# Token columns of the second block multiplied by Strassen-like pairs on the unnormalised input

## The reference, cut to what matters

```python
for l in range(2):
    x = x + 0.5 * swiglu(rms_norm(x, ffn1_norm[l]), ffn1_w_gate[l], ffn1_w_up[l], ffn1_w_down[l])
    u = rms_norm(x, mix_norm[l])
    (a_q, a_k, a_v, b_x, b_b, b_c, c_q, c_kc, c_vc, c_ks, c_vs, c_kw, c_vw, c_g,
     d_q, d_k, d_v, d_g, gate_logits) = jnp.split(u @ w_in[l], SPLIT_POINTS, axis=-1)
    # sliding-window attention (a), short convolution (b), block-sparse attention (c), retention (d)
    ...
    x = x + merged @ w_out[l]
    x = x + 0.5 * swiglu(rms_norm(x, ffn2_norm[l]), ...)
```

## Time and profile before

| | before |
|---|---|
| median of 3 runs | 2752.19 us |
| the profiled execution | 2756.73 us |
| its span on the core | 2754.9 us |
| TensorE busy | 2544.6 us, 92% |
| VectorE busy | 990.4 us, 36% |
| ScalarE busy | 431.9 us, 16% |
| TOK of layer 0 | 1365.90 to 1444.36 us |
| TOK of layer 1 | 2161.39 to 2239.85 us |

### The profile page before, as it was taken

The page is one execution under the profiler, slowest core; times in us unless marked ns, Lnnn a source line. Parts: engine busy times, 40 slices in busy tenths (PEclk is TensorE's granted clock), DMA queues, the critical chain, the costliest instruction groups (busy, mean ns, idle before and its releaser), DMA issues.

```text
span 2754.9 us, 33930 instructions
## 1 busy us (share of the span) xinstructions
PE 2544.6 (92%) x14163; PEld 1950.3 (71%) x14163; DVE 990.4 (36%) x2007; ACT 431.9 (16%) x964; POOL 57.3 (2%) x65
## 2 busy tenths in 40 slices
PE   7998888888878888899999999999999999999999
PEld 5784444444435444588898788888888897788888
DVE  1421100010000001366523522767666325515665
ACT  2321101010111001111012420110110113401110
POOL 0000000000000000100010000000000010000000
PEclk9986877787887788799999999999999999999999
DMA  9657999999999999954565344545544555255440
GB/s 357 241 195 326 420 428 429 428 429 428 428 428 429 428 429 428 380 175 161 154 170 169 106 123 139 182 168 168 172 165 168 154 155 168 80 156 176 154 168 16
DMA packets 250735, 694.43 MB, mean 252 GB/s; under 512 B 11024, under 2 KB 193664, under 8 KB 225536
## 3 DMA queue, kind: packets, MB, share of 16 engines
q1 hardware_dynamic: 248160, 688.54, 67.0%
q10 hardware_dynamic: 2464, 4.32, 0.4%
HBM read 691.78 MB, written 1.05 MB: 251 GB/s over the span
## 4 chain that ended last, share of the span: by engine, by line
PE 84%; DMA 12%; DVE 2%; ACT 1%; issue 1%; SPq 1%; POOL 0%; DVEq 0%
PE banks L1278 11%; DMA ring<-in_w 11%; PE banks L1659 8%; PE banks L1182 7%; PE banks L1198 6%; PE banks L926 4%; PE banks L1742 4%; PE banks L1169 4%; PE banks L1468 3%; PE banks L1335 3%; PE banks L1331 3%; PE banks L1333 3%; PE banks L1337 3%; PE banks L1338 3%; PE banks L1327 3%; PE banks L1329 3%
## 5 line engine op out<-in xcount | busy, mean ns | idle before, releaser
L1169 PE MATMUL banks<-ring,BK 128*32 128x512 f32 x2048 | 274.8, 678 | 127.8 <-DMA ring<-in_w 115.5
L1169 PEld LDWEIGHTS banks<-ring,BK 128*32 128x32 f32 x2048 | 64.8, 117 | 321.9 <-issue 153.9
L1659 PE MATMUL banks<-ZT,ring 128*128 128x256 f32 x1024 | 232.3, 380 | 0.1
L1659 PEld LDWEIGHTS banks<-ZT,ring 128*128 128x128 f32 x1024 | 192.8, 190 | 28.6 <-issue 3.6
L1198 PE MATMUL banks<-ring,GB 128*32 128x512 f32 x976 | 148.9, 754 | 0.0
L1182 PEld LDWEIGHTS banks<-cst,PB 128*128 128x128 f32 x512 | 92.3, 278 | 44.8 <-ACT QT L1931 44.8
L1742 PE MATMUL banks<-YT,ring 128*128 128x256 f32 x512 | 117.3, 380 | 0.0
L1182 PE MATMUL banks<-cst,PB 128*128 128x32 f32 x512 | 94.9, 353 | 24.1 <-DVE QT L2445 24.1
L2445 DVE COPY QT<-banks 128x512 f32<-128x512 f32 x32 | 20.6, 686 | 263.2 <-PE banks L1169 263.2
L926 PE MATMUL banks<-ring,ZT 128*128 128x256 f32 (+2 forms) x576 | 112.4, 358 | 0.0
L1182 PE MATMUL banks<-cst,QT 128*128 128x32 f32 x512 | 111.6, 393 | 0.0
(11 more groups left out here) (460 smaller groups left out, 4004.1 us busy)
## 6 DMA issues: line engine op xcount, KB each, us to landing
ring<-in_w SPq DMA_DIRECT2D x189, 2048.0 KB, 20.3
ring<-in_w_in SPq DMA_DIRECT2D x71, 1024.0 KB, 5.2
ring<-in_ffn_w_gate SPq DMA_DIRECT2D x44, 1024.0 KB, 5.5
ring<-in_ffn_w_up SPq DMA_DIRECT2D x44, 1024.0 KB, 7.8
ring<-in_ffn_w_down SPq DMA_DIRECT2D x44, 1024.0 KB, 5.5
ring<-in_w_mod SPq DMA_DIRECT2D x24, 1024.0 KB, 11.6
ring<-in_w_out SPq DMA_DIRECT2D x12, 1024.0 KB, 5.0
ring<-in_w_branch SPq DMA_DIRECT2D x8, 1024.0 KB, 5.7
```

The source lines that it names most:

```text
L1169: last = mm(ps[32 * j:32 * j + 32, 4 + b, :], XE[:, k, :], slot(n)[:, 512 * b:512 * b + 512], start=(k < 4), stop=(k >= 4))
L1659: last = mm(out, slot(n)[:, 256 * k + P * (c % 2):256 * k + P * (c % 2) + P], ZT[:, k, :], start=(k == 0), stop=(k == KC - 1))
```

## The change

The 12 TOK tiles become six pairs with seven products, like those of an FFN, on the unnormalised input ZG. The pairs are two tiles of one width: 256, 256, 256, 218, 218 and 216. So

- TensorE makes 28 matmuls a pair; the first pair goes through `by_chunks`, the others through the new `tokens(j)`. Both sets of banks are used, and the FEAT tiles go to banks 0 to 6, one each.
- VectorE makes the weight sums of six pairs and the activation sums of ZG, and runs `combine` six times. Those of the first pair stand in the down steps of FFN1.
- ScalarE multiplies each combined result by rstd into PB, 24 instructions a layer in place of eleven evictions of tiles.
- The squares are made per token half (two of 1664) into ZT's storage, each waiting for VectorE's reduction of the one before.
- `rstd_rows` moves from the second tile into the fifth pair, ahead of its product 5; the copy of the rows and the eight multiplications ZG to ZT come after the reductions on VectorE. The sixth pair waits for the copy of the rows, since its product 1 lies in bank 7, and FEAT waits for ZT.
- GpSimd's memset waits until five pairs have been multiplied, and stands ahead of the root of the head sums.
- The ring's slots are freed two at a time at the end of a pair.

```diff
+TOKENS = ((0, 256, 256), (PB_CQ, PB_CQ + 256, 256), (512, PB_KS, 256), (PB_KW, PB_KW + 218, 218),
+          (PB_KW + 436, PB_KW + 654, 218), (PB_KW + 872, PB_KW + 1088, 216))
...
-FFN1, PROJ, FFN2 = 0, 1, 2
+FFN1, PROJ, FFN2, TOK = 0, 1, 2, 3
+ORDER = (FFN1, TOK, PROJ, FFN2)
+NEXT = {1: FFN1, 2: TOK, 0: FFN2}
...
-NEXT_AT = {PROJ: 5, FFN2: PAIRS + 12}
+NEXT_AT = {PROJ: 5, FFN2: PAIRS + 12, FFN1: PAIRS + 12}
...
-        SQ2 = ZP[:, 0:TT * NORMED].rearrange("p (t n) -> p t n", t=TT)
+        SQ2 = ZTf[:, 0:NORMED]
...
         def tile_bank(m):
-            return 2 + m if m < 2 else 4 + m % 4
+            return m - 12
...
+                def tokens(j):
+
+                    nw, ne, w = nth_weights(l, TOK), nth_combined(l, TOK), TOKENS[j][2]
...
+                    if j >= 2:
+                        pe.wait_ge(combined, 4 * (ne + j - 2) + 4)
+                    if j == 5:
+                        pe.wait_ge(rows_copied, l + 1)
+                    for i in (1, 2, 3, 6, 7, 5, 4):
+                        if i == 6:
+                            pe.wait_ge(weights_summed, 4 * nth_summed(l, TOK, j) + 3)
+                        if i == 5 and j == 4:
+                            pe.wait_ge(combined, 4 * (ne + 3) + 4)
+                            rstd_rows()
...
+                by_chunks(TOK, L_TOK, l * 3 + 2, ZG, 256)
+                for j in range(1, len(TOKENS)):
+                    tokens(j)
+                na, nv = l * TILES_A + B1_A, l * TILES_V + B1_V
+                pe.wait_ge(zt_ready, l * KC + KC)
...
+                    if m in (12, 16):
+                        pe.wait_ge(combined, 4 * (nth_combined(l, TOK) + m // 4 + 1) + 4)
...
+                for j, (at1, at2, w) in enumerate(TOKENS):
+                    for n, t, at, c in ((1, 0, at1, E1[:, 0]), (3, 0, at2, E3[:, 0]), (3, 1, at1, E3[:, 1]), (4, 1, at2, E4)):
+                        act.wait_ge(combined, 4 * (ne + j) + n)
+                        last = fn(PB[:, t, at:at + w], c[:, 0:w], ACT.Copy, scale=rcol[:, t:t + 1])
                     last.then_inc(tile_out_a, 1)
...
+                    if j == 3:
+                        act.wait_ge(tile_out_a, na + 4)
+                        for t in range(TT):
+                            act.wait_ge(head_sums, 1 + 2 * l + t)
+                            fn(SQ2, PB[:, t, 0:NORMED], ACT.Square, scale=HD ** -0.5).then_inc(head_squares, 1)
...
-                ffn(FFN1, ZG, vcf("mix"), None)
+                ffn(FFN1, ZG, vcf("mix"), (l, TOK))
...
+                for j, (_, _, w) in enumerate(TOKENS):
+                    if j:
+                        dve.wait_ge(tile_out_a, na + j)
+                    combine(ne + j, pair_set(TOK, j), nw + j, 0, w)
+                    combine(ne + j, pair_set(TOK, j), nw + j, 1, w)
+                    if j == 0:
+                        rstd_diag()
+                    if j + 2 < len(TOKENS):
+                        for part in range(2):
+                            pair_weights(l, TOK, j + 2, part)
+                    if j == 3:
+                        head_square_sums()
+                        normalised()
...
+                pool.wait_ge(sums_used, nth_weights(l, TOK) + 5)
                 nc.gpsimd.memset(YF[:, 2048:3072], 0.0).then_inc(cmp_cleared, 1)
-                pool.wait_ge(head_sums, l + 2)
+                pool.wait_ge(head_sums, 1 + 2 * l + 2)
```

More of the change, by code:

```diff
@@ L82 @@
 STAGES = 3 * NL + 2
-RAW = 3
 V2_LOADS = 21
@@ L131, in nth_summed @@
     if i == 0 and st != PROJ:
-        before = (l, PROJ) if st == FFN2 else (l - 1, FFN2)
+        before = {FFN2: (l, PROJ), TOK: (l, FFN1), FFN1: (l - 1, FFN2)}[st]
         return nth_weights(*before) + NEXT_AT[before[1]]
@@ L1295, in steps, with pair_product @@
                         p4.then_inc(sums_used, 1)
+                def pair_product(st, first, z, w, j, i, k, **kw):
+                    n = U_LAYER + first + 2 * j
+                    one, two = slot(n), slot(n + 1)
+                    even, odd = slice(2 * k * w, 2 * k * w + w), slice(2 * k * w + w, 2 * k * w + 2 * w)
+                    sums, wsum = z_sums(k // 2)[:, k % 2], pair_sums(j)
+                    at = product_out(pair_set(st, j), i)[:, 0:w]
+                    if i == 1:
+                        return mm(at, z[:, 2 * k, 0:P], one[:, even], **kw)
+                    if i == 2:
+                        return mm(at, z[:, 2 * k + 1, 0:P], one[:, odd], **kw)
+                    if i == 3:
+                        return mm(at, sums[:, 3], two[:, odd], **kw)
+                    if i == 4:
+                        return mm(at, z[:, 2 * k + 1, P:T], wsum[:, 2, k, 0:w], **kw)
+                    if i == 5:
+                        return mm(at, sums[:, 0], wsum[:, 0, k, 0:w], **kw)
+                    if i == 6:
+                        return mm(at, sums[:, 1], wsum[:, 1, k, 0:w], **kw)
+                    return mm(at, sums[:, 2], two[:, even], **kw)
@@ L1317, in turn_hidden @@
                         last.then_inc(rows_turned, 1)
[L1319 to L1338, removed]
@@ L1401, in pair @@
                                     pe.wait_ge(acts_summed, 4 * (ns + k // 2) + 4)
-                                last = product(j, i, k, start=(k == 0), stop=(k == 3))
+                                last = pair_product(st, first, ZT, 256, j, i, k, start=(k == 0), stop=(k == 3))
                                 if i == 4 and k < 2:
@@ L1418, in before @@
                             turn_residual(v - 1, 0)
-                    by_chunks() if v > 1 else pair(0)
+                    by_chunks(st, first, v, ZT, 256) if v > 1 else pair(0)
                     for j in range(1, PAIRS):
@@ L2490, in pair_weights @@
                 def pair_weights(at, st, j, part):
[L2492 removed]
+                    first, nth = (L_FFN1, None, L_FFN2, L_TOK)[st] + 2 * j, nth_weights(at, st) + j
                     t_at = at * LAYER_TURNS
@@ L2501, in pair_weights @@
                         else:
-                            dve.wait_ge(sums_used, nth_weights(at - 1, FFN2) + PAIRS)
+                            dve.wait_ge(sums_used, nth_weights(at, FFN1) + PAIRS if st == TOK else nth_weights(at - 1, FFN2) + PAIRS)
                         wait_unit(dve, U_LAYER + first, t_at)
                         wait_unit(dve, U_LAYER + first + 1, t_at)
-                    gate, up = (slot(first + u).rearrange("p (k e n) -> p k e n", k=4, e=2) for u in range(2))
-                    dst = [pair_sums(j)[:, i] for i in range(3)]
+                    w = TOKENS[j][2] if st == TOK else 256
+                    gate, up = (slot(first + u)[:, 0:KC * w].rearrange("p (k e n) -> p k e n", k=4, e=2) for u in range(2))
+                    dst = [pair_sums(j)[:, i, :, 0:w] for i in range(3)]
                     weight_sums(nth_summed(at, st, j), dst, gate[:, :, 0], up[:, :, 0], gate[:, :, 1], up[:, :, 1], part)
```

254 lines of the change are left out of this document (109 added, 145 removed).

## The result

The changed kernel takes 2732.73 us (median of 4 runs, 2730.37 to 2735.26), the kernel before beside it 2753.28 us (4 runs); the ratio is 0.9924, with a 95% interval of 0.9912 to 0.9937. Run again in five rounds it takes 2732.99 us against 2753.36 us, ratio 0.9925 (0.9911 to 0.9939). So 20.4 to 20.6 us are gained, 0.75%.

What follows compares the result with a forecast made beforehand. TOK was taken to be bound by TensorE's columns: 78.46 us a layer becomes 68.47 plus a 0.2 us stall, 9.8 us less. Two layers take 19.6 us off the 2752.19 us median, giving 2732.6 us; range 2729 to 2740 us.

Steps and rivals of the forecast that it cites:

- Price of a matmul and TensorE's queue: TOK on TensorE: 0.4317 us a matmul at 256 columns, 0.3690 at 218, 0.3657 at 216; 68.47 us a layer against 78.46.
- The first pair: Start of TOK: the same sequence elsewhere in the trace takes 12.96 us, and TensorE never waits.
- Sums in FFN1's steps at nothing: First pair's weight sums in FFN1's down steps cost nothing, hidden by VectorE's lead; uncovered 4.66 us a layer.
- The tight place: Before TOK's sixth pair: rows' copy ends at 10.7 us, TensorE wants it at 10.76; stall 0.2 us a layer taken.
- Rival 1: GpSimd's head root locks VectorE out of the multiplications ZG by rows; FEAT 3.4 us a layer late, 2739.4 us; chance 0.13.
- Rival 2: Before the sixth pair: chain of squares 1 to 4 us a layer longer than counted; 2736.6 us at 2 us; chance 0.10.
- Rival 3: TensorE's stall costs clock, 4.9 us lost behind it; slower only from 6.4 us, 2763.4 us at 12 us; chance 0.02.
- Rival 4: TOK: pairs' wait for weight sums or transfers takes the 10 us up again, about 2750 us; chance 0.03.
- Full clock from slice 18 on: Second block: TensorE has its full clock there, so a matmul taken away is worth its full-speed time.
- The sum: Both layers' TOK: 2 x 9.8 = 19.6 us off the median of 2752.19 us gives 2732.6 us.

## Why the prediction was right, point by point

- **Price of a matmul and TensorE's queue.** Predicted 68.47 us without a stall; measured 68.66 with one of 0.24, that is 68.42, and 68.42 us when the wait is taken away. The straight line between widths gave 0.3690 and 0.3657 us; a piece of four is 1.47 and 1.46 us, 0.368 and 0.365.
- **The first pair.** Taking for it was exact: 12.96 us in both layers, no wait.
- **Sums in FFN1's steps at nothing.** Shown twice, at the chosen step and nine steps later.
- **The tight place.** Computed copy of the rows at 10.7 us of the clock that starts with the end of the fourth pair, TensorE at 10.76; measured 1422.15 - 1411.55 = 10.6 and 1422.29 - 1411.55 = 10.74. Stall taken 0.2, measured 0.24 us. The copy ended before TensorE got there, and the piece was still 0.24 us longer: its first weight load, which otherwise lies under the matmul before it, came 0.3 us late (1422.27 us). So the place was tighter than "the two arrive together" says: the weight load wants the copy 0.3 us before the matmul does. With an error of half a microsecond each way on the chain, a hit to 0.04 us is partly luck.
- **Rival 1** fell: the root lets VectorE through. The lock that it supposed is real for another instruction, since additions in the same place hold the multiplications up (7.94 in place of 2.85 us), but three additions did not lengthen TOK.
- **Rival 2** fell: every link of the chain had its duration within 0.1 us. The three scaled copies on ScalarE were done at 1.9 us of the clock and not at 1.6, and that cost nothing, since VectorE was free only at 4.9.
- **Rival 3** did not occur, but its step behind the wait is real. Put at 4.9 us after a 3.4 us wait, it measures 1.9 to 2.9 us after 3.8 and 1.9 us after 1.9. I had argued that 200 us at full clock before the wait speak against it; they don't protect. The 4.9 us were a misreading of the earlier trace rows, which runs two falls together. Cut more finely, the kernel before has

```profile
1153.70:1157.30 3.60, 3.58 (x9) 2.90 (x10) 3.57 (x6) 0.00 (x0) 0.00 (x0) 0.56 1.10 348
1157.30:1160.70 3.40, 3.40 (x19) 3.00 (x17) 3.40 (x4) 0.00 (x0) 0.00 (x0) 1.00 1.10 348
1164.50:1171.10 6.60, 6.60 (x17) 5.29 (x18) 1.50 (x4) 0.51 (x1) 2.18 (x6) 0.54 0.96 304
```

Directly behind the wait of 4.1 us 3.60 x 0.44 = 1.6 us are lost, about what the experiments show; then the clock is full for 3.4 us, and the second fall comes behind a run of short matmuls of 128x2 (32 records). With the eighth product, where the waits there were 0.5 and 0.3 us, the first fall is absent (1.00 from 1150 to 1160 us) and the second is there (0.68 from 1163.5 to 1168.8 us).
- **Rival 4** fell: no wait on a ring slot or a weight sum in TOK.
- **Full clock from slice 18 on.** True of TOK and FEAT (1.00 in both kernels), not of the whole second block: a 9 of the PEclk line stands for 90% or more of a slice of 69 us, and falls of some microseconds in the attention don't show in it. In stretches of 2 us the kernel before has 0.50 at 1526 and 2322 us, the changed kernel at 2298 to 2304 us. The forecast didn't lean on those places.
- **The sum.** 2 x 9.8 = 19.6 us predicted for the two layers and measured as that; the medians moved by 20.4 and 20.6 us. The spans of the profiled executions differ by 21.4 us, and the 1.8 that are over lie ahead of TOK: FFN1's step piece ends at 1360.20 in place of 1362.00 us. In the profiled executions of all runs here that piece ends between 1356.7 and 1362.0 us (at 1357.9 in the kernel before with its squares by halves), so this is spread and not the change. The falls of the clock in the attention, 0 to 3.4 us a layer from one execution to the next, are another part of the spread.
- **Luck.** The medians of 2732.73 and 2732.99 us meet the forecast of 2732.6 more closely than the working earns: the kernel before had 2753.28 and 2753.36 us beside them, not the 2752.19 that the forecast started from, and the gain was 0.8 to 1.0 us larger than 19.6; the two cancel.

## What to carry to other kernels

When the chain of waits lies on TensorE without a gap, a cut in columns is worth its full price: count matmuls by width, take the price of each from a back-to-back stretch of the same trace, and take whole sequences from a place where the program already runs them. Then spend the effort on the one new wait, on a common clock for all engines, because here a stall of 2 us cost 4. And put what another engine waits for (here a copy of 0.4 us) ahead of long work that nobody waits for.

## What the runs showed of the hardware that was not expected

- A TensorE wait of 1.9 us in the middle of a stretch at full clock was followed by 1.9 us of lost clock, one of 3.8 us by 1.9 to 2.9 us, in both layers; the 0.24 us one by none. Waits of 0.9 us in the attention have PEclk 1.00 right around them, but in the same attention, behind short matmuls and a last wait of 0.3 us, the clock fell to half for up to 6.8 us in some executions and not in others.
- A copy that ended 0.14 us before the waiting matmul was due still cost TensorE 0.24 us: the first weight load behind the wait came 0.3 us late.
- GpSimd's power on 128x52 elements (8.7 us) hardly held VectorE's two-input multiplications up (2.85 us for eight, 2.77 in the earlier trace rows), while three additions of 128x1024 (2.0 us each) held them up by 5.1 us.
